# Eight heads of differential attention on eight cores: the next head's projections and the adaLN blocks issued in units between the key steps of the present head

## The chip, the cores and the metric

One Trainium2 chip, all 8 of its cores, one launch. Each core computes its own share with no traffic between cores: two of the 16 prompt sequences (512 context tokens) and half of one of the four latent grids (1024 own tokens; the other 1024 tokens of the same grid are read too, for their keys and values). The metric is the device time of the slowest core in microseconds (us).

## The reference, cut to what matters

```python
sh1, sc1, g1, sh2, sc2, g2 = adaln(c, w_ada, b_ada)          # silu(c) @ w_ada + b_ada, six chunks of 2048
h = rms_norm(x, norm1_w) * (1 + sc1) + sh1
q, k, v, u, g = split(h @ w_in)                              # 1024 columns each, 8 heads of 2 x 64
q = rms_norm(q, q_norm_w); k = rms_norm(k, k_norm_w)         # over 64 dims
q, k = apply_rope(q), apply_rope(k)                          # latent tokens only
p = softmax(q k^T * 64**-0.5)                                # two maps per head, keys: cache + latent
a = p[:, :, 0] - lam * p[:, :, 1]
att = rms_norm(a @ v, subln_w) * (1 - lam_init)
y = x + g1 * (concat(att, spatial_gating(u, g)) @ w_o)
y = y + g2 * (square(relu(modulate(y, sh2, sc2) @ w_ff1)) @ w_ff2)
# state_k, state_v: normed k and v of the context tokens
```

## The kernel before

A helper, `Sched.add` (called `A`), puts each operation on the queue of one engine in the order in which the Python code runs, and puts waits ahead of it for what it reads and overwrites. Each engine works its queue strictly in that order. So the order of the `A` calls is the schedule.

The stages, one after the other with barriers between: (0) adaLN chunks 0 and 1 (shift and scale of the first norm), from eight slabs of `w_adaA`; (1) norm and transpose of 20 tiles of 128 tokens into `hT`, feature-major in bf16, where 512-token block `tb` 0 is the context, 1 and 2 are the own latent tokens, 3 and 4 the others; (2) the heads; (3) spatial gating; (4) output projection, norm and squared-ReLU MLP in two halves of 768 tokens.

The change is inside stage 2, a loop over 8 heads. For a head it first does all projections. Eight blocks (k for `tb` 1 to 4 and 0, q for 1, 2 and 0) go through three stages one step apart. `stA`: `proj_block` (L428, 16 matmuls of 512 columns) and a square on ScalarE. `stB`: a matmul with `bones` that sums over 64 dims (L456), a square root on ScalarE (L458), a reciprocal on VectorE (L459), the multiply into `zn` (L472, L462). `stC`: the matmul with `perm` (L485), then the rotary multiplies and adds on GpSimd (L488, L492, L494) and VectorE (L490, L496). Five blocks of v (`v_block`) are projected feature-major and transposed on TensorE (L621); the context block is projected once more token-major for the `sv` output (L610, 64 matmuls of 128 columns). The weights of a head are three slabs `wsm` of 512 KB, asked for at the head's start, three buffers.

Then `attention` runs three times: query blocks at 512 and 1024 (18 key tiles of 128 each) and the context (two pairs of sequences, 2 key tiles). Each runs twice, for map `c` 0 and 1: two zero matmuls that clear the accumulators `pO` (L516), then per key step the score matmul of the step after next (L529, 512 columns, three PSUM buffers), the exponential (L540) and four matmuls with v (L549, 129 columns). After a map the accumulators are copied (L560), after both a VectorE and ScalarE chain (L565 to L585) makes `on_t`, four transposes put it into PSUM (L593) and ScalarE copies it to `attT` (L596). For the context map, with two key steps, the chain of the block before stands right behind it in the queues. At two places of every 18 key steps `ada_next` issues a block of the remaining adaLN chunks: a load of 1024 KB, and 16 matmuls with 2 stationary and 256 moving columns (L406); after eight blocks, 16 transposes (L375) or a write to `gate_rows`. All 32 blocks are done after the fourth head.

Of the kernel before, what the change touches and what calls it, by code (L numbers as in the profile page):

```python
# [13 lines left out]
D = 2048  # L14
# [3 lines left out]
NTOK = 1536  # L18
# [3 lines left out]

class _Stop(Exception):
    pass

KSTOP = [99]
DBG = {}
# [83 lines left out]
def build_program():  # L111
# [10 lines left out]
    cT = din("cT", [128, 32]); w_adaA = din("w_adaA", [8, 128, 16 * 512]); w_adaB = din("w_adaB", [32, 128, 16 * 256]); bada2 = din("bada2", [2, 6 * D])  # L122
# [25 lines left out]
    try:  # L148
        _body(nc, top, locals())
    except _Stop:  # L150
        pass
    return nc

def _body(nc, top, L):
    globals().update({k: v for k, v in L.items() if k not in ("nc", "top")})
    with top:
# [12 lines left out]
        pT = Ring("pT", [pst(top, "pT%d" % i, [128, 1024], BF16) for i in range(2)])  # L169
# [42 lines left out]

        def chk(phase):
            if KSTOP[0] <= phase:
                S.barrier(engines=("sp",))
                raise _Stop()
# [54 lines left out]
        chk(0)  # L271
# [35 lines left out]
        with ExitStack() as pf:  # L307
# [19 lines left out]
            chk(1)  # L327

            with ExitStack() as pa:
# [3 lines left out]
                wsm = Ring("wsm", [sbt(pa, "wsm%d" % i, [128, 16, 128], BF16) for i in range(3)])  # L333
                qT = sbt(pa, "qT", [128, NTOK], BF16)
                kT = [sbt(pa, "kT%d" % c, [128, NKEY], BF16) for c in range(2)]
                vv = sbt(pa, "vv", [128, 22, 130], BF16)
                ckb = sbt(pa, "ckb", [128, 2, 128], BF16); cvb = sbt(pa, "cvb", [128, 2, 128], BF16)
                sq_ring = Ring("sq", [sbt(pa, "sq%d" % i, [128, 512], BF16) for i in range(2)])
                rs_ring = Ring("rs", [sbt(pa, "rs%d" % i, [128, 512]) for i in range(2)])
                zn_ring = Ring("zn", [sbt(pa, "zn%d" % i, [128, 512], BF16) for i in range(2)])  # L340
                t1_ring = Ring("t1", [sbt(pa, "t1%d" % i, [128, 512]) for i in range(2)])
                t2_ring = Ring("t2", [sbt(pa, "t2%d" % i, [128, 512]) for i in range(2)])
                zf_ring = Ring("zf", [sbt(pa, "zf%d" % i, [128, 512]) for i in range(1)])
                vb_ring = Ring("vb", [sbt(pa, "vb%d" % i, [128, 512], BF16) for i in range(1)])
                so_ring = Ring("so", [sbt(pa, "so%d" % i, [128, 4, 128]) for i in range(1)])
                PT_ring = Ring("PT", [sbt(pa, "PT%d" % i, [128, 512], BF16) for i in range(4)])
                a0_t = sbt(pa, "a0_t", [128, 4, 128])
                o_raw = [sbt(pa, "o_raw%d" % c, [128, 4, 130]) for c in range(2)]
                o_t = sbt(pa, "o_t", [128, 4, 128])
                on_t = sbt(pa, "on_t", [128, 4, 128], BF16)  # L350
                A("dve", lambda e: e.memset(kT[0][64:128, :], 0.0), writes=["kTpad0"])
                A("dve", lambda e: e.memset(kT[1][0:64, :], 0.0), writes=["kTpad1"])
                A("dve", lambda e: e.memset(vv[:, :, 128:130], 1.0), writes=["vones"])
                wa2 = Ring("wa2", [sbt(pa, "wa2%d" % i, [128, 16, 256], BF16) for i in range(2)])
                mch = sbt(pa, "mch", [2, D])

                ada_blocks = [(chunk, blk) for chunk in (3, 4, 2, 5) for blk in range(8)]
                ada_state = {"k": 0, "slots": {}}

                def ada_dma(k):  # L360
                    chunk, blk = ada_blocks[k]
                    wt, wr = wa2.next()
                    ab = (chunk - 2) * 8 + blk
                    A("pool", lambda e: e.dma_start(out=flat(wt[:]), in_=w_adaB[ab, :, :]), writes=[wr], key=wr)
                    ada_state["slots"][k] = (wt, wr)

                def ada_finish(chunk):
                    MCH = [("mch", b) for b in range(8)]
                    if chunk in (3, 4):
                        dst = S2 if chunk == 3 else A2  # L370
                        pt, pr = pS.next()

                        def tr(e):
                            for kc in range(16):
                                ins = e.transpose(pt[:, kc * 2:kc * 2 + 2], mch[0:2, kc * 128:(kc + 1) * 128], identf[0:2, 0:2])  # L375
                            return ins
                        A("pe", tr, reads=MCH + ["identf"], writes=[pr])
                        A("dve", lambda e: e.tensor_copy(out=dst[:].rearrange("p k r -> p (k r)"), in_=pt[:, 0:32]), reads=[pr], writes=[("modc2", chunk)])
                        if chunk == 4:
                            for r in range(2):  # L380
                                A("dve", lambda e, r=r: e.scalar_tensor_tensor(out=A2[:, :, r], in0=A2[:, :, r], scalar=1.0, in1=nw2_t[:], op0=ALU.add, op1=ALU.mult),
                                  reads=[("modc2", 4), "nw2_t"], writes=[("modc2", 4)])
                    else:
                        gi = 0 if chunk == 2 else 1
                        A("sp", lambda e: e.dma_start(out=gsc[2 * gi:2 * gi + 2, :], in_=mch[:]), reads=MCH, key=("gsc", gi))

                def ada_next(n=1):
                    for _ in range(n):
                        k = ada_state["k"]
                        if k >= len(ada_blocks):  # L390
                            return
                        ada_state["k"] = k + 1
                        if k == 0:
                            ada_dma(0)
                        if k + 1 < len(ada_blocks):
                            ada_dma(k + 1)
                        chunk, blk = ada_blocks[k]
                        if blk == 0:
                            A("sp", lambda e: e.dma_start(out=mch[:], in_=bada2[:, chunk * D:(chunk + 1) * D]),
                              writes=[("mch", b) for b in range(8)], key="mch")  # L400
                        wt, wr = ada_state["slots"].pop(k)
                        pt, pr = pg.tiles[1], ("pg", 1)

                        def mm(e):
                            for kc in range(16):
                                ins = e.matmul(pt[0:2, 0:256], lhsT=scT[:, kc, :], rhs=wt[:, kc, :], start=(kc == 0), stop=(kc == 15))  # L406
                            return ins
                        A("pe", mm, reads=[wr, "scT"], writes=[pr])
                        A("dve", lambda e: e.tensor_tensor(out=mch[0:2, blk * 256:(blk + 1) * 256], in0=pt[0:2, 0:256],
                                                           in1=mch[0:2, blk * 256:(blk + 1) * 256], op=ALU.add),  # L410
                          reads=[pr, ("mch", blk)], writes=[("mch", blk)])
# [531 lines left out]
```

How the kernel before makes its waits and increments, by code:

```python
    def _wait(self, eng, sem_name, sem, val):  # L45
        if self.waited[eng].get(sem_name, 0) >= val:
            return
        self.eng[eng].wait_ge(sem, val)
        self.waited[eng][sem_name] = val
# [1 line left out]
    def add(self, eng, fn, reads=(), writes=(), key=None):  # L51
# [15 lines left out]
        ins = fn(self.eng[eng])  # L67
        node = _Node()
        node.eng = eng
        node.dma = key is not None
        if key is not None:
            name = "d_" + str(key)
            if name not in self.dsem:
                self.dsem[name] = self.es.enter_context(self.nc.semaphore(name))
                self.dcnt[name] = 0
            self.dcnt[name] += 1
            ins.then_inc(self.dsem[name], 16)
            node.signal = (name, self.dsem[name], 16 * self.dcnt[name])
        else:
            self.cnt[eng] += 1
            ins.then_inc(self.esem[eng], 1)
            node.signal = ("c_" + eng, self.esem[eng], self.cnt[eng])
        for r in reads:
            self.readers.setdefault(r, []).append(node)
```

## Time and profile before

| what | us |
|---|---|
| three runs | 3406.9, 3635.73, 3752.6; median 3635.73 |
| the profiled execution | 3405.23 |
| its span on the slowest core (all cores 3382.6 to 3404.2) | 3404.2 |
| stage 2, from its first loads to its barrier | 235 to 1447 |
| first projection matmul of a head, heads 0, 1, 5, 6, 7 | 252.5, 406.5, 1012.3, 1153.0, 1293.3 |
| MLP and output projection | 1757 to 3404 |

The page of the profile gives the busy time of each engine and cuts the span in 40 slices. The stage windows tell how busy each engine is in a stretch; the order of TensorE's instructions with the idle time before each tells what it waits for. A matmul of 512 columns is shown with about 0.38 us, but the matmuls overlap: the rate is read from a run of them (16 in 3.62 us, of which the last one's tail is part). TensorE's granted clock is shown as a share of 2.4 GHz; its other level is 1.2 GHz.

### The profile page before, as it was taken

The numbers are of one execution on the slowest core, as the hardware profiler recorded it, in microseconds if no ns is written. First come the engines' busy times: TensorE is split into PE (matmuls) and PEld (weight loads), VectorE is DVE, ScalarE is ACT, GpSimd is POOL, SyncE is SP. The second block draws the span as 40 slices with busy tenths as digits, with TensorE's granted clock in tenths as the row PEclk, the third lists the DMA queues.
The fourth block names the chain that finished last, engine by engine and source line by source line (L and its number), as shares of the span: only waits on it lengthen the run. The fifth ranks groups of instructions, "written<-read, shape, count | busy, mean of one in ns | idle before, by whom it ended". The sixth has DMA issues, their size and how long they took to land.

```text
span 3404.2 us, 53933 instructions; the slowest of 8 cores (3382.6 to 3404.2 us)
## 1 busy us (share of the span) xinstructions
PE 2778.5 (82%) x19656; PEld 1831.7 (54%) x19840; DVE 1181.9 (35%) x2617; ACT 873.2 (26%) x1671; POOL 258.4 (8%) x342
## 2 busy tenths in 40 slices
PE   3437777777867777578987899999997599999998
PEld 1223444444433343334556586868686468686867
DVE  0355344443535435312113332324242414141414
ACT  0472434334253452545110401010100320101010
POOL 0002011111102011000000000000000000000000
PEclk8558888998988999788978899999998799999999
DMA  9651624334111010040136355555557445555555
GB/s 161 161 160 32 107 44 83 64 63 85 31 26 27 1 27 4 4 72 13 26 76 136 62 100 99 100 102 103 104 102 178 95 87 101 103 102 106 100 100 137
DMA packets 65226, 279.56 MB, mean 82 GB/s; under 512 B 11317, under 2 KB 32183, under 8 KB 36792
## 3 DMA queue, kind: packets, MB, share of 16 engines
q0 software_dynamic: 36896, 224.77, 36.9%
q1 hardware_dynamic: 28074, 51.33, 4.8%
q8 instruction: 166, 2.72, 0.3%
q14 instruction: 90, 0.74, 0.1%
HBM read 484.02 MB, written 16.81 MB: 147 GB/s over the span
## 4 chain that ended last, share of the span: by engine, by line
PE 66%; DMA 10%; DVE 10%; ACT 8%; issue 5%; DVEq 0%; ACTq 0%; POOL 0%; SPq 0%; POOLq 0%
PE pg L840 7%; PE pO L840 7%; PE pS L840 7%; PE pg L823 7%; PE pO L823 7%; PE pS L823 6%; PE pO L549 5%; DVE rs L459 5%; PE pg L428 4%; DMA xst<-xs 4%; PE pO L428 4%; DMA wa<-w_adaA 3%; PE pS L529 2%; DMA xst<-xp 2%; PE pg L406 2%
## 5 line engine op out<-in xcount | busy, mean ns | idle before, releaser
L549 PE MATMUL pO<-vv,PT 128*128 128x129 bf16 x2432 | 248.8, 229 | 62.2 <-ACT PT L540 53.1
L828 DVE TENSOR_TENSOR aT<-rl 128x512 bf16<-128x512 bf16 (+1 forms) x256 | 91.9, 359 | 572.7 <-ACT rl L827 572.7
L459 DVE RECIPROCAL rs<-rs 128x512 f32<-128x512 f32 x64 | 214.5, 3352 | 202.1 <-ACT rs L458 202.1
L549 PEld LDWEIGHTS pO<-vv,PT 128*128 128x128 bf16 x2432 | 163.9, 101 | 190.4 <-issue 184.1
L540 ACT ACTIVATE PT<-pS 128x512 bf16<-128x512 f32 x406 | 226.0, 595 | 94.4 <-PE pS L529 60.7
L846 DVE TENSOR_TENSOR acc<-acc,tmp 128x256 f32<-128x256 f32 x384 | 163.3, 425 | 40.0
L292 PE MATMUL pT<-identb,xn 128*128 128x128 bf16 x512 | 61.6, 307 | 130.4 <-DVE hT_own L302 30.5
L428 PE MATMUL pg<-hT_own,wsm 128*128 128x512 bf16 x556 | 140.2, 407 | 30.7 <-DMA wsm<-w_in 21.4
L823 PE MATMUL pO<-h2T,wb 128*128 128x512 bf16 (+1 forms) x946 | 157.9, 325 | 0.7
L840 PE MATMUL pO<-wb,aT 128*128 128x256 bf16 x1344 | 153.6, 273 | 0.0
L840 PE MATMUL pg<-wb,aT 128*128 128x256 bf16 x1344 | 153.6, 273 | 0.0
L840 PE MATMUL pS<-wb,aT 128*128 128x256 bf16 x1344 | 153.6, 273 | 0.0
L529 PE MATMUL pS<-qT,kT 128*128 128x512 bf16 (+1 forms) x386 | 148.3, 403 | 1.3 <-ACT so L442 0.8
L428 PE MATMUL pO<-hT_own,wsm 128*128 128x512 bf16 x556 | 135.1, 397 | 15.7 <-DVE zn L472 10.4
L823 PE MATMUL pS<-h2T,wb 128*128 128x256 bf16 (+1 forms) x880 | 146.7, 325 | 0.8
L840 PEld LDWEIGHTS pO<-wb,aT 128*128 128x128 bf16 x1344 | 131.5, 98 | 15.2
L840 PEld LDWEIGHTS pS<-wb,aT 128*128 128x128 bf16 x1344 | 131.4, 98 | 15.4
L840 PEld LDWEIGHTS pg<-wb,aT 128*128 128x128 bf16 x1344 | 131.3, 98 | 15.5
L823 PE MATMUL pg<-h2T,wb 128*128 128x512 bf16 (+1 forms) x820 | 136.9, 325 | 0.6
L827 ACT ACTIVATE rl<-pO 128x512 bf16<-128x512 f32 x86 | 42.2, 491 | 348.6 <-PE pO L823 348.6
L827 ACT ACTIVATE rl<-pg 128x512 bf16<-128x512 f32 x86 | 42.2, 491 | 348.4 <-PE pg L823 348.4
L827 ACT ACTIVATE rl<-pS 128x512 bf16<-128x512 f32 x84 | 41.2, 491 | 345.0 <-PE pS L823 345.0
(239 smaller groups left out, 4278.1 us busy)
## 6 DMA issues: line engine op xcount, KB each, us to landing
wb<-w_ff POOLq DMA_DIRECT2D x84, 1024.0 KB, 7.9
shr<-w_ff POOLq DMA_DIRECT2D x44, 1024.0 KB, 7.9
wa<-w_adaB POOLq DMA_DIRECT2D x32, 1024.0 KB, 9.6
wa<-w_adaA POOLq DMA_DIRECT2D x8, 2048.0 KB, 30.8
xt<-xs SPq DMA_DIRECT2D x16, 1024.0 KB, 4.9
wsm<-w_in POOLq DMA_DIRECT2D x24, 512.0 KB, 12.5
wb<-w_o POOLq DMA_DIRECT2D x12, 1024.0 KB, 10.5
xst<-xs SPq DMA_DIRECT2D x64, 128.0 KB, 4.9
```

The costliest lines, as they stand in the source:

```text
L292: ins = e.transpose(pt[:, j * 128:(j + 1) * 128], xn[:, kc * 128:(kc + 1) * 128], identb[:])
L406: ins = e.matmul(pt[0:2, 0:256], lhsT=scT[:, kc, :], rhs=wt[:, kc, :], start=(kc == 0), stop=(kc == 15))
L428: ins = e.matmul(pt[:], lhsT=wt[:, kc, :], rhs=hTs(kc, tb * 512, 512), start=(kc == 0), stop=(kc == 15))
L459: A("dve", lambda e: e.reciprocal(out=rs[:], in_=rs[:]), reads=[rsr], writes=[rsr])
L529: ins = e.matmul(ps_[:, a_:a_ + n_], lhsT=kT[c][:, kt * 128:(kt + 1) * 128], rhs=qT[:, q0 + a_:q0 + a_ + n_], start=True, stop=True)
L540: A("act", lambda e, ps_=ps_, P=P: e.activation(out=P[:, 0:nq], in_=ps_[:, 0:nq], func=AF.Exp, scale=0.125), reads=[psr], writes=[Pr])
L549: ins = e.matmul(bank[:, off:off + 129], lhsT=P[:, qi * 128:(qi + 1) * 128], rhs=vv[:, kt, 0:129], start=False, stop=(ki == len(g[2]) - 1) ...
L823: ins = e.matmul(pt[:, 0:cn], lhsT=wcol(wt, kc, fj * 128, 128), rhs=h2T[:, kc, c0:c0 + cn], start=(kc == 0), stop=(kc == 15))
L827: A("act", lambda e, pt=pt, rl=rl, cn=cn: e.activation(out=rl[:, 0:cn], in_=pt[:, 0:cn], func=AF.Relu), reads=[pr], writes=[rlr])
L828: A("dve", lambda e, rl=rl, fc=fc, c0=c0, cn=cn: e.tensor_tensor(out=aT[:, fc, c0:c0 + cn], in0=rl[:, 0:cn], in1=rl[:, 0:cn], op=ALU.mult) ...
L840: ins = e.matmul(pt[:, 0:256], lhsT=aT[:, fc, ti * 128:(ti + 1) * 128], rhs=wcol(wt, fc, 0, 256), start=(fc == 0), stop=(fc == 15))
L846: A("dve", lambda e, tmp=tmp, ti=ti, nb=nb: e.tensor_tensor(out=acc[:, ti, nb * 256:(nb + 1) * 256], in0=acc[:, ti, nb * 256:(nb + 1) * 25 ...
```

## The change

Only stage 2 changes. Per head there are 76 key steps (four times 18, twice 2), now one list over all heads. A generator `fill(h)` holds the projections of head `h` in units: 13 blocks of 4 units (a q or k block: 4 of its 16 matmuls; a v block: the 16 matmuls of 128 columns of one token tile, so v comes out token-major and needs neither the transposes nor the second projection), one unit for the cached keys, and eight adaLN units. In each key step of head `h` the code issues the exponential, up to one unit of head `h + 1` (61 units in 73 steps), the score matmul of the step after next and the four matmuls with v. Head 0's units run ahead of the first key step; in head 7's steps there is only an adaLN unit in every eighth.

What follows a block is posted to run a fixed number of units later (`FP`): square after 1, `bones` matmul after 2, then on ScalarE a logarithm and an exponential with scale -0.5 in place of square root and reciprocal, the multiply after 4, `perm` matmul after 5, rotary after 6 (the add now on VectorE; GpSimd keeps the cosine multiply). The steps after an attention block are posted likewise, one per key step (`MP`), and are issued all at once (`MP.flush`) at the last key step of the next map. One PSUM tile `pm` serves the `bones` matmul, all transposes and the adaLN units; who uses it next first issues the reader of its content. Scores have two PSUM buffers instead of three, blocks have three (`pj`). q is kept zero-padded per map and k unpadded, q, k and v have two sets, `wsm` five slabs. The clearing matmuls are gone (`start=True` on the first step). The cached v goes by DMA straight into `vv`.

The adaLN slabs are cut to 64 of 512 KB, with still two buffers; the load of unit k+2 is posted two units after unit k. The first 32 units have the weights stationary and 2 moving columns; the last 32 have 2 stationary and 128 moving columns, a small load of the bias each and a small write to `gate_rows`.

```diff
-                wsm = Ring("wsm", [sbt(pa, "wsm%d" % i, [128, 16, 128], BF16) for i in range(3)])
+                wsm = Ring("wsm", [sbt(pa, "wsm%d" % i, [128, 16, 128], BF16) for i in range(5)])
+                wa2 = Ring("wa2", [sbt(pa, "wa2%d" % i, [128, 16, 128], BF16) for i in range(2)])
...
+                s_ring = Ring("pS", [pS.tiles[0], pS.tiles[1]])
+                pj_tiles = [pg.tiles[0], pg.tiles[1], pTf[1]]
+                pm, pmb, pmr = pTf[0], pTb[0], ("pT", 0)
...
+                def pm_free():
+                    fn, pm_held[0] = pm_held[0], None
+                    if fn is not None:
+                        fn()
+
+                def pm_use(emit, consume):
+                    pm_free()
+                    emit()
+                    pm_held[0] = consume
+                    FP.post(1, lambda: pm_free() if pm_held[0] is consume else None)
...
+                def ada_unit():
...
+                        def mm(e):
+                            for kc in range(16):
+                                ins = e.matmul(pm[:, 0:2], lhsT=wt[:, kc, :], rhs=scT[:, kc, :], start=(kc == 0), stop=(kc == 15))
+                            return ins
...
+                        gi = ci - 2
+                        mt, mr = mch.next()
+                        A("sp", lambda e: e.dma_start(out=mt[:], in_=badaG[gi, :, j * 128:(j + 1) * 128]), writes=[mr], key=mr)
...
+                                ins = e.matmul(pm[0:2, 0:128], lhsT=scT[:, kc, :], rhs=wt[:, kc, :], start=(kc == 0), stop=(kc == 15))
...
+                        def fin():
+                            A("dve", lambda e: e.tensor_tensor(out=mt[:], in0=pm[0:2, 0:128], in1=mt[:], op=ALU.add), reads=[pmr, mr], writes=[mr])
+                            A("sp", lambda e: e.dma_start(out=gsc[2 * gi:2 * gi + 2, j * 128:(j + 1) * 128], in_=mt[:]), reads=[mr], key=("gsc", k % 2))
...
+                    if k + 2 < 64:
+                        FP.post(2, lambda: ada_dma(k + 2))
...
-                    A("act", lambda e: e.activation(out=rs[:], in_=p2[:], func=AF.Sqrt, bias=epsc[:, 0:1], scale=1.0), reads=[p2r, "epsc"], writes=[rsr])
-                    A("dve", lambda e: e.reciprocal(out=rs[:], in_=rs[:]), reads=[rsr], writes=[rsr])
+                        A("act", lambda e: e.activation(out=rs[:], in_=pm[:], func=AF.Ln, bias=epsc[:, 0:1], scale=1.0), reads=[pmr, "epsc"], writes=[rsr])
+                        A("act", lambda e: e.activation(out=rs[:], in_=rs[:], func=AF.Exp, scale=-0.5), reads=[rsr], writes=[rsr])
...
+                    for d, fn in ((1, c1), (2, c2), (4, c4), (5, c5), (6, c6)):
+                        FP.post(d, fn)
...
+                    yield from blk("k", 1)
+                    yield from vgrp(1)
+                    yield from blk("k", 2)
+                    if h + 1 < 8:
+                        w_dma(h + 1, "k")
+                        w_dma(h + 1, "q")
+                        c_dma(h + 1)
+                    yield from vgrp(2)
+                    yield from blk("q", 1)
+                    yield from cache()
+                    yield from vgrp(0)
+                    yield from blk("k", 0)
+                    yield from ada(3)
+                    yield from blk("q", 2)
+                    yield from vgrp(3)
+                    yield from blk("k", 3)
+                    yield from vgrp(4)
+                    yield from blk("k", 4)
+                    if h + 1 < 8:
+                        FP.post(3, lambda: w_dma(h + 1, "v"))
+                    yield from ada(3)
+                    yield from blk("q", 0)
+                    yield from ada(2)
+                    FP.flush()
...
+                for si, (h, q0, groups, c, ki, n) in enumerate(steps):
+                    p = h % 2
+                    MP.tick()
+                    ps_, psr = s_of.pop(si)
+                    P, Pr = PT_ring.next()
+                    A("act", lambda e, ps_=ps_, P=P: e.activation(out=P[:], in_=ps_[:], func=AF.Exp, scale=0.125), reads=[psr], writes=[Pr])
+                    want = ((si % NS) + 1) * FILL_UNITS // (NS - 3)
+                    while h + 1 < 8 and 0 <= filled[h + 1] < want:
+                        if not pull(h + 1):
+                            break
+                    if h == 7:
+                        FP.tick()
+                        if si % 8 == 3:
+                            ada_unit()
+                    s_mm(si + 2)
...
+                    A("pe", av, reads=[Pr, ("vones", p)] + [("vv", p, g[2][ki] // 4) for g in groups], writes=pO_res)
+                    if ki == n - 1:
+                        MP.flush()
```

## Rows read from the trace of the kernel before

**Rows 1.** The page: span, and each engine's busy time, share and instructions.
```profile
span 3404.2 us, 53933 instructions; the slowest of 8 cores (3382.6 to 3404.2 us)
PE 2778.5 (82%) x19656; PEld 1831.7 (54%) x19840; DVE 1181.9 (35%) x2617; ACT 873.2 (26%) x1671; POOL 258.4 (8%) x342
```

**Rows 2.** Stage windows: start:end and length, busy time of each engine, clock, DMA share, GB/s.
```profile
core 2: us, PE busy (x) PEld busy (x) DVE busy (x) ACT busy (x) POOL busy (x), PEclk, DMA share, GB/s
404.00:1447.00 1043.00, 777.89 (x5362) 420.35 (x5454) 461.71 (x845) 421.07 (x790) 142.07 (x139) 0.89 0.21 38
1870.00:3404.00 1534.00, 1445.00 (x11136) 1096.76 (x11200) 496.49 (x1239) 181.60 (x382) 70.30 (x133) 0.97 0.54 104
```

**Rows 3.** The same windows for head 6 (projections, then attention) and head 7's attention.
```profile
1153.00:1233.00 80.00, 59.50 (x315) 28.35 (x319) 48.77 (x68) 18.47 (x31) 17.92 (x17) 0.91 0.07 14
1233.00:1293.00 60.00, 44.07 (x392) 26.18 (x401) 14.96 (x48) 41.01 (x82) 0.22 (x1) 0.90 0.12 21
1372.00:1447.00 75.00, 47.98 (x399) 28.50 (x404) 20.20 (x64) 44.23 (x86) 1.11 (x2) 0.80 0.02 5
```

**Rows 4.** TensorE in order, projections of heads 0 and 1: start, us, [idle before <-releaser].
```profile
252.52 4.05 PE L428 MATMUL pg<-hT_own,wsm 128*128 128x512 bf16 x9 [21.37 <-DMA wsm<-w_in]
...
422.14 0.59 PE L485 MATMUL pS<-zn,perm 128*128 128x512 bf16 x1 [3.80 <-DVE zn L472]
422.51 6.32 PE L428 MATMUL pg<-hT_own,wsm 128*128 128x512 bf16 x16
...
443.17 3.62 PE L428 MATMUL pg<-shr,wsm 128*128 128x512 bf16 x16
```

**Rows 5.** Groups of instructions, whole span: busy us, mean ns of one, idle before.
```profile
L540 ACT ACTIVATE PT<-pS 128x512 bf16<-128x512 f32 x406 | 226.0, 595 | 94.4 <-PE pS L529 60.7 <-PE pO L516 19.4 <-PE pg L406 12.6
L459 DVE RECIPROCAL rs<-rs 128x512 f32<-128x512 f32 x64 | 214.5, 3352 | 202.1 <-ACT rs L458 202.1
L458 ACT ACTIVATE rs<-pS,epsc 128x512 f32<-128x512 f32 x64 | 43.6, 681 | 0.1
L472 DVE SCALAR_TENSOR_TENSOR zn<-pO,qkw_t,rs 128x512 bf16<-128x512 f32 x24 | 18.0, 751 | 3.1 <-DVE rs L459 1.4
```

**Rows 6.** The chain that ended last: start, us, what.
```profile
308.06 3.57 PE pS L610 x64
```

**Rows 7.** TensorE in order inside head 0's attention.
```profile
344.52 0.63 PE L549 MATMUL pO<-vv,PT 128*128 128x129 bf16 x8
...
347.55 0.88 PE L549 MATMUL pO<-vv,PT 128*128 128x129 bf16 x8 [0.46 <-ACT PT L540]
...
348.52 0.39 PE L549 MATMUL pO<-vv,PT 128*128 128x129 bf16 x4
...
350.54 0.39 PE L549 MATMUL pO<-vv,PT 128*128 128x129 bf16 x4
350.85 1.91 PE L406 MATMUL pg<-wa,scT 128*2 128x256 bf16 x16
```

**Rows 8.** All engines in order: an adaLN transpose, a block's end chain, the stage's tail.
```profile
393.37 1.12 PE L375 MATMUL pS<-identf,mch 2*128 2x2 f32 x16 [0.67 <-DVE mch L409]
...
402.86 0.59 PE L593 MATMUL pT<-identb,on_t 128*128 128x128 bf16 x4 [4.34 <-DVE on_t L585]
...
1435.49 0.77 DVE L560 COPY o_raw<-pO 128x260 f32<-128x260 f32 x2 [2.97 <-PE pO L549]
...
1443.89 0.60 ACT L596 ACTIVATE attT<-pT 128x512 bf16<-128x512 bf16 x1 [2.07 <-PE pT L593]
```

**Rows 9.** DMA issues by line: KB each, median us to landing.
```profile
wa<-w_adaB POOLq DMA_DIRECT2D x32, 1024.0 KB, 9.6
...
wu<-w_in POOLq DMA_DIRECT2D x8, 512.0 KB, 5.1
...
sv<-so SPq DMA_DIRECT2D x8, 256.0 KB, 2.3
```

**Rows 10.** DMA issues between 1220 and 1240 us (head 7's three weight slabs).
```profile
wsm<-w_in POOLq DMA_DIRECT2D x3, 512.0 KB, 7.8
```

More of the change, by code:

```diff
@@ L339, in _body @@
[L339 to L344, printed above, removed]
@@ L360, in ada_dma @@
+                ada_slots = {}
+                ada_i = [0]
                 def ada_dma(k):
-                    chunk, blk = ada_blocks[k]
                     wt, wr = wa2.next()
[L363 to L402, printed above, removed]
+                    A("pool", lambda e: e.dma_start(out=flat(wt[:]), in_=w_adaB[k, :, :]), writes=[wr], key=wr)
@@ new lines, in blk_chain, with c1, c2 @@
+                    st = {}
+                    def c1():
+                        sq, sqr = tb_ring.next()
+                        A("act", lambda e: e.activation(out=sq[:], in_=pt[:], func=AF.Square), reads=[pr], writes=[sqr])
+                        st["sq"] = (sq, sqr)
+                    def c2():
+                        sq, sqr = st["sq"]
+                        pm_use(lambda: A("pe", lambda e: e.matmul(pm[:], lhsT=bones[:], rhs=sq[:], start=True, stop=True), reads=[sqr, "bones"], writes=[pmr]), c3)
@@ new lines, in _body @@
+                FILL_UNITS = 4 * 13 + 1 + 8
+                steps = []
+                for h in range(8):
+                    for (q0, lat) in ((512, True), (1024, True), (0, False)):
+                        groups = [(0, 4, list(range(4, 22)))] if lat else [(0, 2, [0, 1]), (2, 2, [2, 3])]
+                        for c in range(2):
+                            n = len(groups[0][2])
+                            for ki in range(n):
+                                steps.append((h, q0, groups, c, ki, n))
@@ new lines, in _body, with pull, drain @@
+                fills = {h: fill(h) for h in range(8)}
+                filled = [0] * 9
+                def pull(h):
+                    if h >= 8 or filled[h] < 0:
+                        return False
+                    try:
+                        next(fills[h])
+                        filled[h] += 1
+                        return True
+                    except StopIteration:
+                        filled[h] = -1
+                        return False
+                def drain(h):
+                    while pull(h):
+                        pass
```

537 lines of the change are left out of this document (264 added, 273 removed).

## The prediction

> **What bounds the kernel now.** I read the page first. TensorE is busy for 82% of the span, VectorE for 35%, ScalarE for 26% [rows 1], so TensorE is the engine to look at, and the question is in which stage it idles. The stage windows answer that. In the MLP TensorE is busy 1445 of 1534 us at a granted clock of 0.97; between 404 and 1447 us, seven heads of the stage that the change rewrites, it is busy only 778 of 1043 us at 0.89, with VectorE at 462 and ScalarE at 421 [rows 2]. No engine is full there: engines wait for each other.
>
> The windows of one head show two halves. The projections of head 6 take 80 us and its attention 60 [rows 3]. At the full level of the clock a block of 16 matmuls of 512 columns goes by in 3.45 us (3.62 less the tail of the last) [rows 4], so 13 blocks are 45 us, and the rest of the 80 is the second v projection (3.6 us [rows 6]), small matmuls and waits. The order of TensorE's instructions shows such a wait: 3.80 us for `zn`, and behind it 16 matmuls took 6.32 us instead of 3.62, because the clock had fallen to its 1.2 GHz level [rows 4]. Behind `zn` stands the reciprocal: 64 times 3.35 us, 27 us of VectorE per head [rows 5]. In attention a key step costs 0.505 us (four steps from 348.52 to 350.54 [rows 7]), so 76 steps are 38 of the 60 us. The turn from one map to the next costs 2.4 us from the last four v matmuls of one (they end at 345.15) to the first of the next (347.55) [rows 7], and the short context map waits 4.34 us for `on_t` [rows 8].
>
> **The work of a head after the change.** In the changed kernel one queue of TensorE holds the key steps of head h and the units of head h+1, so I price a head by TensorE's own time and then add what it must wait for.
> - 13 blocks at 3.45 us: 44.9. The token-major v costs the same: 64 matmuls of 128 columns took 3.57 us [rows 6].
> - A key step: 16 of 512 columns in 3.45 make 0.216 for the scores, 4 of 64 in 3.57 make 0.223 for v, 0.44 together; 76 of them 33.4.
> - 8 `bones` and 6 `perm` matmuls at 0.216: 3.0. Transposes of `on_t`, of the context k and of the cached keys: 1.8 (three fours at 0.22, and 1.1 for the rest).
> - 8 adaLN units. 16 matmuls of 2 columns took 1.12 us [rows 8]; 16 of 64 v matmuls of 128 columns would be 0.9 [rows 6]. I take 1.0 for either form: 8.0. Before, a block was 1.84 (1.91 less a tail [rows 7]) and there were 8 in each of four heads.
> - In 15 of the 76 steps there is no unit, and the exponential sets the 0.505 us [rows 7]: 1.0 more.
>
> Sum: 92.1 us. ScalarE has 76 exponentials spaced 0.5 us (38), eight times square, logarithm and exponential (about 0.6 + 0.68 + 0.6, by the rows of L540 and L458 [rows 5]: 15) and some 7 us of copies: 60 us. VectorE loses the 27 us of reciprocals. Neither reaches 92, and both have a step of slack: the exponential of a step may run while TensorE does the unit and the v matmuls of the step before. So they cost nothing by themselves; without that cover a step would cost the 0.505 again plus its unit.
>
> **What TensorE waits for in a head.** These are the terms that I had to choose.
> - *The third adaLN unit of a run of three.* There are two slab buffers, so the load of unit k+2 can't start before unit k's matmuls end, and unit k+2 stands two units later in TensorE's queue. Until there TensorE has two key steps and a unit, 1.9 us. A slab of 512 KB landed 5.1 us after its issue in the gating stage [rows 9]. So TensorE stops for 3.2 us, and with it the scores, v matmuls and exponentials behind. In the second run of three the v slab of the next head goes out first on the same queue: three slabs asked for together have a median of 7.8 us [rows 10], so the second lands some 3.3 us after the first, at 8.4. TensorE has three key steps and two units until then, 3.3 us: a stop of 5.1. The last run has two units and a whole block before them: nothing. Together 8.3. Bounds: 0 if slabs landed in time; if they land as `wa` did (9.6, 1024 KB [rows 9]), 7.7 and, a slab later, 10, together 18. I take the row of the same size. The Trainium skill prices such a load lower (DMA: Bandwidth & Descriptors, anatomy of one DMA: about 2 us fixed and the bytes at 436 GB/s, which is 3.2 us for 512 KB); by that, an estimate, the two stops would be 1.3 each, 2.6 in place of 8.3, and the time 40 us less, but the 5.1 measured in this kernel decides.
> - *The flush.* The context map has two steps, so the chain of the block before is issued at once behind step 74, with its transposes in TensorE's queue. It waits as today: 4.3 us [rows 8].
> - *The clock.* Each of these three stops is as long as the 3.80 us behind which 16 matmuls took 2.7 us too long [rows 4]: 3 times 2.8 = 8.4. Bounds: 0, and 15.
> - *The turn of a map.* The copy of `pO` (0.77 us [rows 8]) now lies beside a unit of 0.86 and the scores: 0.3 each for six, 2 (bounds 0 and 11, today's price without cover).
> - *The chain behind a block.* From `bones` to `perm` there are three units, some 3.9 us; the chain is 0.4 + 0.68 + 0.6 + 0.75 [rows 5] and the hand-overs, 2.8, plus what ScalarE and VectorE are busy with. `pm` is shared too: an adaLN unit behind a `bones` matmul waits for the logarithm. I take 0.5 for each of 8 blocks, 4 (bounds 0 and 12).
> - For the last 32 adaLN units (three and a half heads) the next use of `pm` waits for a bias load through SyncE, which stands behind a write that waits for VectorE. A small transfer landed in 2.3 us [rows 9]. Four us in each of three heads: 12 in all (bounds 0 and 30).
>
> A head: 92.1 + 8.3 + 4.3 + 8.4 + 2 + 4 = 119. Seven such heads and the 12: 845 us.
>
> **The two ends of the stage.** The first block needs the k slab, which is now asked for first and not second: start at 249 rather than 252.5 [rows 4]. Head 0's 53 units without key steps: 45 + 2.5 of small matmuls and 3 of waits, 51 (today 75). Head 7 has only the key steps, bound by ScalarE. With two score buffers a score waits for the exponential two steps before; I take 0.57 a step for today's 0.505, 43 us, adaLN units 8, turns 6, flush and clock 7, and the same tail of 9 us (from 1435.5 to 1444.5 [rows 8]): 73, today 75 [rows 3].
>
> Sum: 249 + 51 + 845 + 73 = 1218, where today the stage ends at 1447. That is 229 less; the other stages are not touched. 3405 - 229 = 3176 us. The three runs shown spread from 3406.9 to 3752.6 with a median 1.068 times the profiled 3405.23; the sum is made against the profiled one, and the upper end of the range carries that spread.
>
> **The rivals.**
> 1. *Clean overlap.* The slabs land in time and chains cost nothing: 119 - 8.3 - 5.6 of clock - 4 = 101 a head, 3176 - 126 - 12 = 3040 us. Against it: two buffers fix the order of load and use.
> 2. *Loads and chains are later.* The slabs land like `wa`, and each chain costs 1.5 us: 10 + 8 more a head, 126 in all: 3300 us. For it: the same channels carry weights for all eight cores, and 7.8 is a median of three. Against it: the stage moves little data.
> 3. *The waits move into the one queue.* Each of eight blocks stops TensorE at `perm` as `zn` does today, 3.8 us and 2.7 of clock: 52 a head instead of 4, about 336: 3512 us, slower by 3%. Without the reciprocal the chain is 2.4 us of work and not 5.2, which speaks against it. A third of that price leaves 3290; two thirds, within 2%.
> 4. *Slower: the clock.* If the small stops between unit, scores and v matmuls kept TensorE at its 1.2 GHz level for most of a head, the 92 us would be 184: 7 times 84 more (the 8.4 are in it): 3760 us. It decides from 33 us more a head on, a third of the matmuls at the low level. Against it: attention today, with gaps in every step, runs at a step of 0.505 and matmuls of full rate [rows 7], and its window shows 0.90 [rows 3]. The Trainium skill (TensorE: Matmul & The Clock Gate, a second HAM failure mode) tells of a kernel whose short idle times between groups of matmuls through cycled PSUM banks made the clock swing between its levels; by that rule this rival would be the outcome, and the trace does not agree for the steps of today.
>
> **How the numbers follow.** Forecast 0.56 (own range 3090 to 3290), rival 1 0.15, rival 2 0.17, rival 3 0.08, rival 4 0.04. A difference of 2% is about what can be told from no change here. Rivals 1 and 2 and the forecast are faster by more than that, and so is a quarter of rival 3: 0.90. Half of rival 3 is within 2%: 0.04. Its last quarter and rival 4 are slower: 0.06. The range must hold 8 in 10: from 3080 (part of rival 1 is below) to 3400 (rival 2, and the forecast times 1.068).
>
> **What the profile after would show.** The stage ends near 1218 us; a head from first unit to first unit is 119 us; TensorE's busy share in it rises from 75% to over 80%. Two waits on `wa` per head of 3 and 5 us, on the third unit of a run, and one for `on_t` of 4; the clock falls behind each. No reciprocal of 512 columns and no table load within the heads. Head 7 at about 0.57 a step. The prediction is wrong if the waits on `wa` are missing, if the wait at `perm` stands among the longest, or if the clock in the stage is under 0.85.

## The result, and the profile after

The changed kernel takes 3173.24 us (median of four runs, three of them within 3170.86 to 3174.51); the predicted time was 3176. Its runs stand to those of before at 0.9318, 95% interval 0.9291 to 0.9345: 6.8% less time. In some runs the cores of one die are slower, whatever the kernel: every ratio and comparison below leaves them out, so that of some experiments a single run counts.

The page of the kernel after, for [rows 1]:

```profile
span 3169.8 us, 56807 instructions; the slowest of 8 cores (3140.3 to 3169.8 us)
PE 2671.6 (84%) x21261; PEld 1882.6 (59%) x21472; DVE 960.7 (30%) x2458; ACT 903.4 (29%) x1697; POOL 205.0 (6%) x326
```

The busy share of TensorE rose from 82% to 84% of a shorter span; VectorE lost 221 us of work, 214.5 of it the reciprocals [rows 5]. The stage windows of the kernel after follow, for [rows 3]: heads 0 (its projections alone), 1, 5 (each from one set of cached-v loads to the next, so one head's key steps with the next head's units) and 7 (key steps alone). Columns as there.

```profile
core 4: us, PE busy (x) PEld busy (x) DVE busy (x) ACT busy (x) POOL busy (x), PEclk, DMA share, GB/s
257.00:306.60 49.60, 46.02 (x438) 29.97 (x441) 14.92 (x22) 18.74 (x29) 9.29 (x11) 1.00 0.33 63
421.80:538.10 116.30, 94.24 (x977) 64.35 (x993) 37.20 (x99) 63.06 (x115) 14.58 (x21) 0.90 0.31 57
892.30:1012.20 119.90, 100.28 (x981) 69.81 (x996) 38.25 (x101) 63.73 (x116) 14.35 (x20) 0.93 0.31 55
1132.00:1218.00 86.00, 55.88 (x531) 38.20 (x538) 29.86 (x98) 45.80 (x87) 3.17 (x6) 0.83 0.26 43
```

A head takes 115 to 122 us where projections and attention took 140 one after the other [rows 3]. TensorE is busy for 81 to 84% of it. The waits of TensorE between 306 and 1130 us, seven heads together, are these (engine, tile and line; what it waited for; us in total, times, longest):

```profile
PE pT L423 <- DMA wa<-w_adaB: 24.5, 7, 5.8
PE pS L657 <- ACT PT L726: 20.2, 11, 4.2
PE pO L743 <- DVE o_raw L750: 19.5, 27, 0.8
PE pT L441 <- DMA wa<-w_adaB: 13.7, 3, 5.6
PE pT L423 <- ACT tf L468: 11.5, 9, 3.2
PE pT L441 <- DVE o_t L680: 9.9, 3, 3.3
PE pT L423 <- DVE o_t L680: 9.5, 3, 3.2
PE pT L441 <- ACT tf L468: 6.2, 6, 1.1
```

L423 and L441 are the adaLN matmuls of the narrow form (2 moving columns) and of the wide form (128), L657 the scores, L743 the v matmuls, L464 `bones`. The `perm` matmul (L495), behind whose wait for `zn` the clock had fallen before [rows 4], is not in the list: the chain of a block is covered.

The name `o_t` in this list misleads. In this core's trace 57 weight loads of `bones` stand between 306 and 1130 us but only 48 of their matmuls: the other records are missing, and an adaLN unit behind such a gap seems to have waited alone. Core 3 has all 56 of both, and no wait for `o_t`. The end of head 1's steps there:

```profile
522.92 0.76 DVE L750 COPY o_raw<-pO 128x258 f32<-128x258 f32 x2 [3.21 <-PE pO L743]
...
524.27 0.15 DVE L426 TENSOR_TENSOR S<-pT,badaT_t 128x2 f32<-128x2 f32 x1
524.57 0.38 PE L464 MATMUL pT<-tbf,bones 128*128 128x512 bf16 x1 [1.76 <-DVE S L426]
525.15 0.69 ACT L468 ACTIVATE tf<-pT,epsc 128x512 f32<-128x512 f32 x1 [2.45 <-DVE o_t L680]
525.98 0.54 PE L423 MATMUL pT<-scT,wa 128*128 128x2 bf16 x16 [1.04 <-ACT tf L468]
```

VectorE reads an adaLN unit's result out of `pm` (L426) only after the copy of the accumulators and the first steps of the finish chain. The `bones` matmul needs `pm` and waits 1.76 us for that, and the next adaLN unit waits 1.04 us for the logarithm. So the adaLN units wait for their slab and for the logarithm that still reads `pm`; what waits for the chain of the attention block is the reader of `pm`, and behind it `bones`.

### The profile page after: what moved, and what is told of

It is laid out like the page before. It is cut to its first block, busy times and chain, and to the rows that moved or that the text cites. A ratio compares the mean times of both kernels' runs of the same rounds, so it can differ in the third digit from the quotient of the medians.

```text
span 3169.8 us, 56807 instructions; the slowest of 8 cores (3140.3 to 3169.8 us)
## 1 busy us (share of the span) xinstructions
PE 2671.6 (84%) x21261; PEld 1882.6 (59%) x21472; DVE 960.7 (30%) x2458; ACT 903.4 (29%) x1697; POOL 205.0 (6%) x326
## 4 chain that ended last, share of the span: by engine, by line
PE 72%; DMA 13%; ACT 5%; DVE 5%; issue 4%; POOL 0%; DVEq 0%; ACTq 0%; SPq 0%; POOLq 0%
PE pg L916 7%; PE pO L899 7%; PE pO L916 7%; PE pS L916 7%; PE pg L899 7%; PE pS L899 7%; PE pg L537 5%; DMA xst<-xs 5%; PE pO L743 5%; PE pS L657 3%; DMA wa<-w_adaA 3%; PE pg L552 3%; PE pT L537 2%; DMA wa<-w_adaB 2%; PE pT L552 2%
## 5 line engine op out<-in xcount | busy, mean ns | idle before, releaser
L726 ACT ACTIVATE PT<-pS 128x512 bf16<-128x512 f32 x608 | 350.9, 595 | 256.7 <-PE pS L657 219.4
L743 PE MATMUL pO<-vv,PT 128*128 128x129 bf16 x2432 | 254.4, 231 | 29.8 <-DVE o_raw L750 23.0
L743 PEld LDWEIGHTS pO<-vv,PT 128*128 128x128 bf16 x2432 | 198.2, 103 | 136.8 <-issue 52.9
L657 PE MATMUL pS<-qz,kT 128*128 128x512 bf16 (+1 forms) x556 | 214.4, 396 | 32.0 <-ACT PT L726 30.8
L899 PEld LDWEIGHTS pO<-h2T,wb 128*128 128x128 bf16 x960 | 93.9, 98 | 62.1
L279 PEld LDWEIGHTS pT<-identb,xn 128*128 128x128 bf16 x512 | 49.2, 136 | 133.7 <-issue 131.4
```

The source lines that it names most:

```text
L279: ins = e.transpose(pt[:, j * 128:(j + 1) * 128], xn[:, kc * 128:(kc + 1) * 128], identb[:])
L657: ins = e.matmul(ps_[:, a_:a_ + n_], lhsT=kT[p][:, kt * 128:(kt + 1) * 128], rhs=qz[p][c][:, q0 + a_:q0 + a_ + n_], start=True, stop=True)
L726: A("act", lambda e, ps_=ps_, P=P: e.activation(out=P[:], in_=ps_[:], func=AF.Exp, scale=0.125), reads=[psr], writes=[Pr])
L743: ins = e.matmul(pO[qi // 2][:, off:off + 129], lhsT=P[:, qi * 128:(qi + 1) * 128], rhs=vv[p][:, kt, 0:129], start=(ki == 0 and qi % 2 == ...
L899: ins = e.matmul(pt[:, 0:cn], lhsT=wcol(wt, kc, fj * 128, 128), rhs=h2T[:, kc, c0:c0 + cn], start=(kc == 0), stop=(kc == 15))
```

## Experiments: the two halves of the change, each without the other

The first question is which half the 232 us come from. Three kernels answer it: the norm alone, the interleaving with the old norm, and the new code with nothing interleaved.

**The norm alone**, in the kernel before:

```diff
-                    A("act", lambda e: e.activation(out=rs[:], in_=p2[:], func=AF.Sqrt, bias=epsc[:, 0:1], scale=1.0), ...
-                    A("dve", lambda e: e.reciprocal(out=rs[:], in_=rs[:]), ...
+                    A("act", lambda e: e.activation(out=rs[:], in_=p2[:], func=AF.Ln, bias=epsc[:, 0:1], scale=1.0), ...
+                    A("act", lambda e: e.activation(out=rs[:], in_=rs[:], func=AF.Exp, scale=-0.5), ...
```

> The kernel before with one edit: logarithm and exponential on ScalarE in place of square root and reciprocal in the block norm. Theory (TensorE's queue is the bound, the chain behind a block counts only where the queue waits for it): VectorE loses 27 us per head, but TensorE idles only some 20 us in the 80 us of a head's projections, and about 12 of them go: eight heads 80 to 110 us, 3300 to 3325 us. Rival (the norm is the change, the interleaving adds little): the chain is the whole idle time, 20 to 27 us per head, 3190 to 3245 us.

Measured: 3287 us (3286.1 and 3287.5), ratio to before 0.9656 (0.9614 to 0.9697). 118 us, 15 a head, a little over the theory's 80 to 110 and well short of the rival's. TensorE's waits for `zn`, 40.5 us in seven heads of the kernel before, are gone from the list. Another wait shows the working. TensorE's wait of the context-k transposes for `zf`, in seven heads, first in the kernel before and then in this one:

```profile
PE pS L438 <- DVE zf L462: 66.8, 7, 9.5
```

```profile
PE pS L438 <- DVE zf L462: 29.0, 7, 4.1
```

It is shorter by 5.4 us a head, which is two reciprocals of 3.35 us less two exponentials of 0.6: two blocks' norms stand in a row there. It is not gone, because the chain stays serial whoever computes it.

**The interleaving with the old norm:** the same two lines the other way round, in the changed kernel.

> The changed kernel with square root and the VectorE reciprocal back in the block norm, all else as it is. Theory: the chain from the bones matmul to the perm matmul grows by 2.7 us and by two table loads of 1.28 us to some 8 us and has 3.9 us of cover, so each of eight blocks stops TensorE by about 4 us, and the clock falls behind it: 30 to 50 us a head, 3400 to 3520 us. Rival (the interleaving hides the reciprocal): under 10 us a head, below 3240 us.

Measured: 3409 to 3432 us in eight runs (median 3413), ratio to before 1.0034 (1.0008 to 1.0060). The interleaving with the old norm gains nothing at all. The theory's range held, its place for the cost only in part, as the waits will show. The groups of this kernel that load activation tables, and its waits at `perm` between 324 and 1340 us:

```profile
L726 ACT ACT_TABLE_LOAD x57 | 73.1, 1283 | 1.0
L468 ACT ACT_TABLE_LOAD x56 | 71.8, 1283 | 56.6 <-PE pT L464 56.1
```

```profile
PE pg L495 <- DVE tbf L475: 30.8, 18, 1.8
PE pT L495 <- DVE tbf L475: 16.5, 10, 1.8
```

In the kernel before square roots and exponentials were apart, and there were 7 and 8 loads at these places. Interleaved, each of the 56 blocks after the first head's needs two, 145 us of ScalarE in all, and in this queue each also delays the exponential of a key step:

```profile
640.05 1.28 ACT L468 ACT_TABLE_LOAD   x1 [0.89 <-PE pT L464]
641.35 0.69 ACT L468 ACTIVATE tf<-pT,epsc 128x512 f32<-128x512 f32 x1
642.05 1.28 ACT L726 ACT_TABLE_LOAD   x1
643.35 1.09 ACT L726 ACTIVATE PT<-pS 128x512 bf16<-128x512 f32 x2
```

TensorE now waits at `perm` 28 times, up to 1.8 us, 47 us in all. The theory had put about 4 us at each block there. All its waits in seven heads are 281 us, on the same core of the changed kernel 129: the scores wait 57 us for the exponential instead of 21, the adaLN units 67 for the readers of `pm` instead of 23, the transposes of the finish chain 35 instead of 11. A middle head takes 146 us, and the granted clock in it is 0.84. So the interleaving pays only with the new norm: the norm is worth 118 us in the old code and 240 in the interleaved. Which part of the 240 is the reciprocal and which the table loads no run separates.

**The new code, nothing interleaved:** the units of a head in one piece between two heads.

```diff
-                    while h + 1 < 8 and 0 <= filled[h + 1] < want:
+                    while False:
```

> The changed kernel with all units of a head issued in one piece between two heads, none between key steps. Theory: 50 us of blocks as head 0 takes, some 16 for adaLN units whose slabs now have less cover, and 66 for 76 bare key steps with turns and flush: 132 a head instead of 117, about 3280 us. Rival (the interleaving is nearly the whole gain): a head as before, 140 to 155 us, 3340 to 3440 us. Rival (the norm is the whole gain): below 3200 us.

Measured: 3373.6 and 3380.9 us, 200 above the changed kernel; the theory's 3280 missed by nearly 100, and the first rival held. A head takes 147 us, of which key steps and units:

```profile
451.00:520.00 69.00, 49.11 (x391) 31.16 (x399) 20.00 (x66) 43.45 (x82) 0.00 (x0) 0.85 0.05 8
520.00:598.00 78.00, 58.04 (x588) 37.51 (x595) 17.50 (x32) 21.49 (x35) 14.37 (x19) 0.87 0.43 78
```

The theory gave 66 and 66. Most of the error is in the units: 50 us for the blocks, as in head 0, and 16 for the adaLN units were too little. In this head there are two slab waits (4.9 and 5.5 us), three waits of 1.0 for the logarithm, and a clock at 0.87 where head 0 of the changed kernel had 1.00. So the new code without the interleaving is 90 us slower than the old code with the new norm, and the interleaving covers that and 114 us more. It has two score buffers for three, one `pm` for many users, and its key steps take 69 us where the whole attention of a head took 60 [rows 3]; how the 90 us divide among these no run shows. Nor was the new code run with the old norm and nothing interleaved, so how much of the step from 118 to 240 us is the interleaving itself stays open.

| | old norm | new norm |
|---|---|---|
| projections ahead of attention, old code | 3405 | 3287 |
| the same, new code | not run | 3377 |
| interleaved | 3413 | 3173 |

## Experiments: what the remaining waits cost

**Without the adaLN units.**

> The changed kernel without the adaLN units and their slab loads (the second norm then gets scale 1 and shift 0, and the gates only the bias: part of the computation is left out). Theory: per head 8 units of 0.5 to 1.6 us, the slab wait of 5.6, about 3 us of waits at the shared PSUM tile and the clock behind: 15 a head and 12 in head 7, 3050 us. Rival (they fill idle time): within 20 us of the changed kernel.

Measured: 3077 us, ratio 0.9040 (0.9014 to 0.9067): 96 us for 64 units, of which some 50 are their own matmuls by the rows below. The theory said 123, the rival under 20. The head still has its stop at the end of attention: now the transposes of the finish chain wait there, up to 5.6 us, for the logarithm that reads `pm` (37.5 us in seven heads), and this logarithm stands in ScalarE's queue behind the chain.

**The adaLN units one by one** between blocks, instead of runs of three, three and two:

```diff
+                    yield from ada(1)      # after each of v2, v0, v3, q2, v4, k3
...
-                    yield from ada(3)      # after k0
-                    yield from ada(3)      # after k4
+                    yield from ada(1)
-                    yield from ada(2)      # after q0
+                    yield from ada(1)
```

The v blocks 3 and 4 also move ahead of q2 and k3, to stand between units.

> The changed kernel with the eight adaLN units of a head one by one between blocks, never two in a row; as many units, the same two slab buffers. Theory: the slab wait (5.6 us) and the clock behind it go, and part of the waits at the shared PSUM tile: 7 to 10 us a head, 3100 to 3125 us. Rival (the second run's wait is the load channel's, not the distance of two units): waits of several us on wa stay, 3160 us or more.

Measured: 3131 us (four runs within 1.1 us), ratio 0.9197 (0.9176 to 0.9217): 42 us, 6 a head, a little less than the theory's 7 to 10. The longest waits of TensorE between 310 and 1130 us, on core 5:

```profile
PE pS L662 <- ACT PT L731: 34.8, 26, 3.9
PE pO L748 <- DVE o_raw L755: 23.9, 34, 0.8
PE pT L706 <- DVE mch L445: 20.1, 3, 6.8
PE pT L706 <- DVE A L426: 13.7, 2, 7.0
PE pT L706 <- DVE S L426: 13.4, 2, 6.7
```

No wait for a slab is left in the view: the distance of two units was the cause, and with the same two buffers it is cured by order alone. But the transposes of the finish chain (L706) now wait 6.6 to 7.0 us in each head, 47 in all, where they had waited 8 to 11 in all. Part of that had lain in the waits of the `bones` matmul and of the adaLN units.

**Partial flush.** At the last step of a map only the posted steps that read `o_raw` are issued:

```diff
-                        MP.post(d, fn)
+                        MP.post(d, fn, d <= 3)
...
                     if ki == n - 1:
-                        MP.flush()
+                        MP.run_tagged()
```

> The changed kernel in which the last key step of a map issues only those posted steps that read the copied accumulators; the others of the finish chain keep their one-per-step places. Theory: the three waits of together 7.5 us around the context map go, and the low clock behind them: 8 to 10 us in each of seven heads, 3100 to 3120 us. Rival (the copy of the accumulators for the next map waits for VectorE anyway, the wait only changes its place): within 15 us of the changed kernel.

Measured: 3166 and 3169 us, ratio 0.9303 (0.9276 to 0.9330), which can't be told from the changed kernel. Waits of TensorE in seven heads, on core 3 of the changed kernel and then on core 3 of this one, whose line numbers are 5 higher:

```profile
PE pO L743 <- DVE o_raw L750: 20.0, 28, 0.8
PE pT L464 <- DVE mch L445: 9.8, 6, 1.9
PE pT L701 <- DVE A L426: 4.4, 2, 2.2
```

```profile
PE pO L748 <- DVE o_raw L755: 21.1, 31, 0.9
PE pT L469 <- DVE mch L450: 10.1, 6, 2.2
```

The transposes' waits, 10.5 us in all in the changed kernel, are gone from the list, and half of it comes back at other places (the turns of the maps, the transposes of the context k). The wait of the `bones` matmul is what it was: the steps that read `o_raw` are still issued at once, and the reader of `pm` stands behind them. The wait of the scores for the exponential does not fall either (18.6 and 20.7 us). So the rival held in its figure. From the loads for head 1 to those for head 7 the eight cores take 4 us less on average, so the edit has a small gain.

**No flush at the end of a head's units.** That unchanged wait has another cause. All engines of the changed kernel in order, at the start of head 2:

```profile
541.53 0.74 DVE L475 SCALAR_TENSOR_TENSOR tf<-pT,qkw_t,tf 128x512 f32<-128x512 f32 x1
542.37 1.28 ACT L484 ACTIVATE qz<-tf 64x512 bf16<-64x512 f32 x2 [2.88 <-DVE tf L475]
543.67 1.08 ACT L726 ACTIVATE PT<-pS 128x512 bf16<-128x512 f32 x2
...
544.41 0.58 PE L657 MATMUL pS<-qz,kT 128*128 128x512 bf16 x1 [2.47 <-ACT PT L726]
```

The last block's steps are flushed, so two copies into q (L484) stand on ScalarE ahead of the next exponentials and wait 2.88 us for VectorE. Their q is first read 70 steps later. The edit:

```diff
-                    FP.flush()
+                    if h == 0:
+                        FP.flush()
```

> The changed kernel without the flush at the end of a head's units (the last q block's steps keep their places in the next head's key steps; only head 0 flushes). Theory: ScalarE's two copies into q no longer stand ahead of the next head's exponentials while they wait for VectorE; the stop of 2.5 us at the scores and the low clock behind it go: 3 to 4 us in each of seven heads, 3143 to 3155 us. Rival (VectorE's finish chain holds the queue, whoever stands there): within 8 us of the changed kernel.

Measured: 3150.5 and 3151.9 us, profiled 3154.7, ratio 0.9262 (0.9247 to 0.9278): some 20 us, 3 a head, as the theory said. The wait of the scores for the exponential went from 20.2 to 7.4 us in seven heads; the rest of the gain was not traced to a place.

**Four score buffers in the last head.**

```diff
+                s_tiles = [pS.tiles[0], pS.tiles[1], pg.tiles[0], pg.tiles[1]]
...
-                    ps_, psr = s_ring.next()
+                    sl = si % (4 if h == 7 else 2)
+                    ps_, psr = s_tiles[sl], s_names[sl]
```

> The changed kernel with four score buffers instead of two in the last head, where the block buffers are idle. Theory: a bare key step goes from 0.64 us, as the trace of the changed kernel shows it, to the 0.505 of before: 72 steps, 8 to 10 us: 3163 to 3166 us. Rival (the exponential alone sets the step, 0.595 us each): under 3 us.

Measured: 3167.6 us in one run, 1.6 above the theory's range, which times alone can't tell from no change. The traces can: from the loads for head 7 to the first loads of the next stage the eight cores take 199 us on average where the changed kernel's take 204. The v matmuls of bare key steps in head 7, first of the changed kernel and then of this one:

```profile
1162.53 0.39 PE L743 MATMUL pO<-vv,PT 128*128 128x129 bf16 x4
...
1163.85 0.39 PE L743 MATMUL pO<-vv,PT 128*128 128x129 bf16 x4
...
1165.12 0.39 PE L743 MATMUL pO<-vv,PT 128*128 128x129 bf16 x4
```

```profile
1161.22 0.39 PE L745 MATMUL pO<-vv,PT 128*128 128x129 bf16 x4
...
1164.31 0.39 PE L745 MATMUL pO<-vv,PT 128*128 128x129 bf16 x4
```

Two steps lie from each of the first three lines to the next, 1.27 to 1.32 us, so 0.65 a step. Six steps lie between the last two, 0.515 a step. That is under the 0.595 of one exponential, against the rival. At three turns of the maps some of it is given back (waits of 0.8 us for the exponential).

**All of it.** First the adaLN units one by one with the partial flush, and ten units in each of six heads and four in the seventh, so that the last has none:

> Both edits at once (adaLN units one by one, partial flush), and ten adaLN units in each of seven heads so that the last head has none. Theory: the two gains add, and the last head loses eight units of 1.9 us with their waits while the seven others take one more each: 3030 to 3060 us. Rival (each gap closed opens the next wait in the same queue): 3090 us or more.

Measured: 3086 us in one run, between the theory's 3060 and the rival's 3090. Alone the edits had given 42 us and nothing measurable; with the emptied last head they give 87. The loads of the cached v mark the heads, and between the second and the last of them (six heads) the partial flush took 3 us off the changed kernel (705.7 to 702.8) but 21 off the one with single units (655.7 to 634.6), though it had twelve units more there. The cores agree on both figures: on average 4 and 22. The traces suggest why. The transposes' wait, which the partial flush takes away, was 1.5 us a head in the changed kernel and 7 with single units; in the new kernel (core 1) it is gone and 24 us stand at the `bones` matmul, up to 4.0 each. But the places of the units changed too, and no run has single units with the partial flush alone. Then with the two later edits too (the flush at the end of a head's units stays for heads 0 and 7):

> All edits in one kernel: adaLN units one by one and none in the last head, partial flush, no flush at the end of a head's units, four score buffers in the last head. Theory: 3086 of the three together, less 3 us in each of seven heads and 9 in the last: 3050 to 3060 us. Rival (the waits around the context map only change their place): 3070 us or more.

Measured: 3060.4 to 3065.2 us in five runs, ratio to before 0.9000 (0.8986 to 0.9013), just above the theory's range. This kernel beats both: 10.0% under the kernel before and 3.4% under the changed one. Its seven interleaved heads (and part of the last) in one window:

```profile
304.00:1100.00 796.00, 710.94 (x7468) 483.93 (x7466) 286.63 (x763) 483.79 (x891) 102.06 (x135) 0.94 0.34 60
```

## Why the prediction was right, point by point

The time was right within 3 us, and that is in part luck. Misses cancelled: the seven heads took 20 us less than forecast, the first units and the last head 20 more. And cores differ by more than 3 us: from the kernel before to the changed one the first loads of the next stage come 214 to 247 us earlier, core by core. Their mean is 229, as forecast.

**What bounds the stage.** Right. A head is TensorE's queue plus its waits: 117.9 us on average between 306.6 and 1132 us, where I had 119 and, with the bias loads, 121 (825 us for the seven, predicted 845). The matmul terms need one correction. The narrow adaLN unit passes in less than the 1.0 us that I took from a transpose of fp32 data: 16 matmuls in 0.54. The wide one was right at 1.05. That makes 88.4 us in place of 92.1 in the first four heads, and the 4 us between the two forms are most of why heads 4 to 6, with the wide form, take 120 to 122 us and those before them 115 to 116.

```profile
515.18 0.54 PE L423 MATMUL pT<-scT,wa 128*128 128x2 bf16 x16
...
516.14 0.38 PE L464 MATMUL pT<-tbf,bones 128*128 128x512 bf16 x1
517.61 0.54 PE L423 MATMUL pT<-scT,wa 128*128 128x2 bf16 x16 [1.09 <-ACT tf L468]
...
524.18 0.56 PE L423 MATMUL pT<-scT,wa 128*128 128x2 bf16 x16 [5.56 <-DMA wa<-w_adaB]
524.60 0.59 PE L657 MATMUL pS<-qz,kT 128*128 128x512 bf16 x1
```

**The slab waits.** This is the second run of three in head 1's steps. The third unit waits 5.56 us for its slab (3.6 to 5.8 in the seven heads) and the scores behind it run at 1.2 GHz, as predicted (5.1 us, the v slab ahead on the same queue). But the first run's wait, predicted at 3.2 us, was 1.5, 0.4 and 0.5 in three heads and none in four; on four of the eight cores it never came. The step that failed is "until there TensorE has two key steps and a unit, 1.9 us": the shared tile makes the `bones` matmul and the unit behind it wait for VectorE and for the logarithm, about 2.5 us in that place, and in this time the slab lands. The wait was there, under another name. In sum the slabs cost 38.2 us in seven heads, 29 to 37 on the other cores, predicted 58.

**The flush.** Predicted 4.3 us a head for `on_t`; measured 7: 2.9 at the `bones` matmul and the adaLN unit behind it (the waits that the list calls `o_t`), 1.2 at the transposes, 2.9 of scores behind ScalarE. The wait was predicted at the transposes, and there it is short. I had not seen that the flush at the end of the units meets the flush of the finish chain on VectorE. In the experiment without the first the scores' wait fell, and those at `bones` and at the transposes stayed at some 27 and 10 us in seven heads (on cores whose records are whole): these were two causes.

**Turns and chains.** 2.8 us a head at the turns (predicted 2), and 4.5 for the logarithm and the readers of `pm` (predicted 4, though I had put it at `perm`, which never waited long). The bias loads held VectorE (21 us between 770 and 1220 us), not TensorE.

**The clock.** The windows of the interleaved heads show 0.90 to 0.93 where I had feared under 0.85 as a sign of error; only the last head, with no units, is below, at 0.83. At 0.90 a fifth of 116 us is at the low level, so it costs at most 12 us; what is left of a head's 118 after matmuls, waits and the wide units is 8, predicted 8.4. This term is a remainder, and no experiment measured it alone. Where the clock fell two windows of head 1's steps show:

```profile
440.00:476.00 36.00, 34.66 (x381) 24.54 (x385) 8.27 (x14) 23.12 (x42) 5.48 (x7) 1.00 0.21 40
524.00:545.00 21.00, 12.95 (x125) 8.46 (x128) 9.01 (x28) 9.20 (x17) 2.35 (x4) 0.74 0.56 95
```

In the first, key steps and units follow each other with short idle times only and the clock stays at 2.4 GHz. The second stands right behind a slab wait of 5.56 us, and three more waits of 1.8 to 3.2 lie in it.

**The ends.** Start at 250 (predicted 249), the first units until 306.6 (predicted 300), the last head until about 1219 (predicted 73 us, measured 87). One failed step there is the 0.57 us a key step with two buffers: it is 0.64, 5 us in all. The other 9 us stand where 7 were predicted for flush and clock: the list of that stretch has three waits of 2.2 to 2.7 us of the scores for the exponential and one of 5.2 for `on_t` at the context map, and from 1135 to 1152 us key steps pass at the low clock, 0.86 us each. The stage ends at 1219 us, predicted 1218: too much for the seven heads, too little for the ends. The rest of the kernel took 1951 us in place of 1957, which is within the spread of the cores of the kernel before (1949 to 1962).

**The rivals.** The clean overlap was 3040 us; what came nearest to it, the last kernel, is at 3063, with the edits that remove the waits it named and two more. Rival 4, the clock, did not come. The Trainium skill's rule (TensorE: Matmul & The Clock Gate, a second HAM failure mode), that short idle times between matmul groups through cycled PSUM banks make the clock swing, does not agree with the window at 1.00 above. Rival 3, stops at `perm`, is what the kernel with the old norm shows in part; there they are 1.8 us and not 3.8.

## What to carry to other kernels

When independent work is woven into another stage's queue, price it as one queue: the sum of both streams' matmuls, plus each wait at the place where it stands. An operation may not pay off before the weaving and be its condition afterwards: here the norm without square root and reciprocal was worth 118 us in the old code and 240 once the streams shared ScalarE, its activation tables and VectorE. Before you trust the name of a wait, compare it with a core whose records are whole. Look for work that is issued early without need (a flush, a load two units ahead, a shared PSUM tile): it stands ahead of somebody in a queue. And expect that removing one wait shows the next one in the same place; the edits paid together what they did not pay alone.

## What the runs showed of the hardware

Alternating square root with exponential on ScalarE cost 113 table loads of 1283 ns in the interleaved stage; with logarithm and exponential the stage had one, at its start. The Trainium skill (ScalarE: Activation LUTs, Table sets: the hidden batching unit) says that logarithm and exponential share a set and that square root has another. The trace agrees. For a switch it gives about 2.7 us (same page, What ACT_TABLE_LOAD costs): 1283 ns of load and some 1380 of a drain. The load agrees; the drain is not in the rows above, where 1.3 us pass from the end of one activation to the start of the next. A key step with scores, exponential and four v matmuls ran at 0.64 to 0.65 us with two score buffers and at 0.515 with four (0.505 with three, in the kernel before), while one exponential is shown with 0.595: successive ones overlap, if their input is there in time.
